# Turning the first mixer's tiles by DMA instead of on TensorE

## What is computed

```python
proj = h @ w_in                      # stick-breaking q,k,v; conv input (2 x 512); gla q,k,v,r; gates
w   = exp(log_sigmoid(z) + reverse_cumsum(log_keep) - log_keep)   # z = q k^T * 64**-0.5, 8 heads
sb  = w @ v                                                       # stick-breaking attention
u   = a * sigmoid(g);  y = depthwise_conv(u, conv_w)              # 31 taps over time, 512 channels
conv = silu(layer_norm(y))
S   = chunk_decay * S + k_dec^T v;  o = (q * 64**-0.5) @ S        # gated linear attention, 4 heads
gla = rms_norm(o) * silu(r)
m   = sum(sigmoid(gate_i) * (branch_i @ w_branch_i)) @ w_out
```

## Time and profile before

| | |
|---|---|
| median of 3 runs (lowest, highest) | 2055.99 us (2055.59, 2056.20) |
| the profiled execution, its own time | 2055.71 us |
| its span in the trace | 2053.9 us |
| busy: TensorE, VectorE, ScalarE | 2036.4, 1385.7, 1120.8 us |
| granted TensorE clock, mean | 0.999 |

### The profile page before, as it was taken

The page is one execution under the profiler, slowest core; times in us unless marked ns, Lnnn a source line. Parts: engine busy times, 40 slices in busy tenths (PEclk is TensorE's granted clock), DMA queues, the critical chain, the costliest instruction groups (busy, mean ns, idle before and its releaser), DMA issues.

```text
span 2053.9 us, 24653 instructions
## 1 busy us (share of the span) xinstructions
PE 2036.4 (99%) x9886; PEld 1683.2 (82%) x9886; DVE 1385.7 (67%) x1801; ACT 1120.8 (55%) x1386; POOL 0.2 (0%) x4
## 2 busy tenths in 40 slices
PE   8999999999999999999999999999999999999998
PEld 6888887888888888887888888898888888988887
DVE  6666798766657666798776656866665668566564
ACT  6445657664446445666564446646644466565443
POOL 0000000000000000000000000000000000000000
PEclk9999999999999999999999999999999999999999
DMA  8765654456766675554567655443576554445763
GB/s 273 210 205 170 208 177 145 167 193 203 217 200 205 208 212 169 196 171 144 180 212 211 212 175 200 164 145 135 179 219 206 181 197 156 149 143 186 204 217 113
DMA packets 302193, 382.69 MB, mean 186 GB/s; under 512 B 74672, under 2 KB 210176, under 8 KB 302080
## 3 DMA queue, kind: packets, MB, share of 16 engines
q1 hardware_dynamic: 298112, 369.88, 56.8%
q10 hardware_dynamic: 3968, 11.24, 1.6%
HBM read 365.86 MB, written 1.05 MB: 179 GB/s over the span
## 4 chain that ended last, share of the span: by engine, by line
PE 97%; DMA 1%; ACT 1%; DVE 1%; issue 0%; SPq 0%; DVEq 0%; ACTq 0%
PE ps L541 86%; PE ps L1072 2%; PE ps L609 1%; PE ps L632 1%; PE ps L1175 1%; PE ps L1156 1%; DMA raw<-in_ffn_w_up 1%; DVE x L1846 1%; PE ps L805 1%; DMA raw<-in_w_in 0%; PE ps L690 0%; PE ps L1020 0%; ACT w_hi L1234 0%; PE ps L986 0%; PE ps L650 0%
## 5 line engine op out<-in xcount | busy, mean ns | idle before, releaser
L1805 DVE TENSOR_TENSOR w_lo<-raw,w_hi 128x2048 fp32r<-128x2048 f32 x342 | 773.4, 2266 | 308.9 <-ACT w_hi L1234 307.7
L1234 ACT ACTIVATE w_hi<-raw 128x2048 fp32r<-128x2048 f32 x342 | 648.0, 1897 | 448.1 <-PE ps L541 327.2
L541 PE MATMUL ps<-w_hi,hT_hi 128*128 128x512 f32 x2000 | 788.9, 394 | 1.8 <-DVE w_lo L1805 1.8
L541 PE MATMUL ps<-w_lo,hT_hi 128*128 128x512 f32 x2000 | 779.7, 390 | 0.0
L541 PE MATMUL ps<-w_hi,hT_lo 128*128 128x512 f32 x2000 | 757.7, 391 | 0.0
L541 PEld LDWEIGHTS ps<-w_hi,hT_hi 128*128 128x128 f32 x2000 | 375.9, 188 | 83.9 <-issue 6.6
L541 PEld LDWEIGHTS ps<-w_hi,hT_lo 128*128 128x128 f32 x2000 | 375.2, 188 | 78.8
L541 PEld LDWEIGHTS ps<-w_lo,hT_hi 128*128 128x128 f32 x2000 | 376.1, 188 | 74.6
L541 PE MATMUL ps<-w_hi,bT_hi 128*128 128x512 f32 x640 | 250.9, 392 | 0.0
L541 PE MATMUL ps<-w_hi,bT_lo 128*128 128x512 f32 x640 | 249.3, 389 | 0.0
L541 PE MATMUL ps<-w_lo,bT_hi 128*128 128x512 f32 x640 | 249.2, 389 | 0.0
(11 more groups left out here) (298 smaller groups left out, 1312.6 us busy)
## 6 DMA issues: line engine op xcount, KB each, us to landing
raw<-in_w_in SPq DMA_DIRECT2D x160, 512.0 KB, 4.5
raw<-in_ffn_w_gate SPq DMA_DIRECT2D x88, 512.0 KB, 3.7
raw<-in_ffn_w_up SPq DMA_DIRECT2D x88, 512.0 KB, 4.7
raw<-in_ffn_w_down SPq DMA_DIRECT2D x88, 512.0 KB, 4.3
raw<-in_w_gate SPq DMA_DIRECT2D x44, 512.0 KB, 3.7
raw<-in_w_up SPq DMA_DIRECT2D x44, 512.0 KB, 4.7
raw<-in_w_down SPq DMA_DIRECT2D x44, 512.0 KB, 4.2
raw<-in_w_out SPq DMA_DIRECT2D x32, 512.0 KB, 4.4
```

The costliest lines, as they stand in the source:

```text
L541: mm = nc.tensor.matmul(bank(t, half), act[:, tiles[i], t * P:(t + 1) * P], w, start=start and (i, n) == steps[0], stop=stop and (i, n) == ...
L1234: nc.scalar.activation(w_hi[:, u % HIGH_RING, cols], raw[:, slot, cols], ACT.Copy).then_inc(high_ready, 1)
L1805: V.tensor_tensor(w_lo[:, slot, cols], raw[:, slot, cols], flat(w_hi[:, u % HIGH_RING, cols]), ALU.subtract).then_inc(low_ready, 1)
```

## The change

Three sets of tiles no longer pass through TensorE: the convolution's input, the linear attention's queries, and the stick-breaking queries and keys. VectorE parts each into 16-bit planes (`part_planes`), SP turns the planes with two DMA transposes (`turn_planes`, one for each `t`), and VectorE joins them (`join_planes`). Two transposes of 512 columns of 16 bits serve the linear attention's queries, as in the feed-forward blocks; the other three take two of 1024 columns. SP issues them in its load queue, after a wait for VectorE's planes. The scales that went with the copies out of PSUM (0.5 and 1/8) go into the evictions, by `rstd_half` and a new column `rstd_eighth`. The squares of the linear attention's output move from VectorE to ScalarE: eight Square activations of 128 columns with an accumulator, ahead of the root. Some taps change places on VectorE; their number is the same.

```diff
 SyncE, in the mixer's load loops (k is the unit after the one just issued)
+                    if k == U_FFN + 10:
+                        sp.wait_ge(*after("conv_glu", "planes", l))
+                        turn_planes(conv_planes_T, conv_planes, conv_turned)
+                    if k == U_FFN + 13:
+                        sp.wait_ge(*after("gla_decay", "planes", l))
+                        turn_planes(gq_planes_T, gq_planes, gla_q_turned)
...
+                        if k == U_FFN + 18:
+                            sp.wait_ge(*after("sb_planes", "q", l))
+                            turn_planes(sb_planes_T, sb_planes, sb_turned)
+                        if k == U_FFN + 20:
+                            sp.wait_ge(*after("sb_planes", "k", l))
+                            turn_planes(sb_planes_T, sb_planes, sb_turned)
 TensorE
-            steps = {("conv_g", 1): [gla_alpha], ("gla_qk", 0): [conv_turn], ("gla_v", 0): [gla_decays],
-                     ("gla_r", 0): [gla_updates], ("sb_q", 0): [gla_reads],
-                     ("sb_k", 0): [sb_turn_q], ("sb_k", 1): [gla_turn], ("sb_v", 0): [sb_turn_k]}
+            steps = {("conv_g", 1): [gla_alpha], ("gla_v", 0): [gla_decays], ("gla_r", 0): [gla_updates],
+                     ("sb_q", 0): [gla_reads], ("sb_k", 1): [gla_turn]}
 ScalarE
         def gla_std(l):
-            act.wait_ge(*after("gla_out", "sums", l))
+            act.wait_ge(*after("gla_out", "rows", l))
+            for h in range(8):
+                cols = slice(h * P, (h + 1) * P)
+                nc.scalar.activation(gsq_f[:, cols], go_f[:, cols], ACT.Square,
+                                     accum_out=ssg[:, h:h + 1]).then_inc(*done("gla_std", f"sum{h}"))
+            act.wait_ge(*after("gla_std", "sum7", l))
             nc.scalar.activation(stdg, ssg, ACT.Sqrt, bias=EPS, scale=1.0 / P).then_inc(*done("gla_std", "std"))
...
                 if name == "sb_k":
                     gla_std(l)
-                    act.wait_ge(*after("sb_turned", "q", l))
-                    copy(sbqT, two(4), "sb_in", "qT", 64 ** -0.5)
                 if name == "sb_v":
                     gla_out(l)
-                    act.wait_ge(*after("sb_turned", "k", l))
-                    copy(sbkT, two(4), "sb_in", "kT")
 VectorE
+        def part_planes(dst, src):
+
+            return V.tensor_copy(dst, src.bitcast(U16).rearrange("p t (n b) -> p t b n", b=2))
+
+        def join_planes(dst, src):
+
+
+            for t in range(TT):
+                joint = V.tensor_copy(dst.bitcast(U16).rearrange("p c (n b) -> p b c n", b=2)[:, :, :, t * P:(t + 1) * P],
+                                      src[:, t, :, :].rearrange("p (b c) n -> p b c n", b=2))
+            return joint
...
+        def sb_join(l, which):
+            dve.wait_ge(sb_turned, l * 64 + (32 if which == "q" else 64))
+            join_planes(sbqT if which == "q" else sbkT, sb_planes_T).then_inc(*done("sb_planes", which + "T"))
...
-            V.tensor_tensor(gsq_f, go_f, go_f, ALU.mult).then_inc(*done("gla_out", "squares"))
-            dve.wait_ge(*after("gla_out", "squares", l))
-            V.tensor_reduce(ssg, gsq_f.rearrange("p (h v) -> p h v", h=8), AX.X, ALU.add).then_inc(*done("gla_out", "sums"))
...
             weight_low(L, k + 9)
             conv_in(l)
-            taps(1)
+            taps(2)
             weight_low(L, k + 10)
+            gla_q_planes(l)
             taps(2)
...
             weight_low(L, k + 15)
             gla_rows(l)
+            sb_part(l, "q")
             weight_low(L, k + 16)
             gla_gated(l)
-            taps(2)
+            taps(1)
+            sb_join(l, "q")
             weight_low(L, k + 17)
+            sb_part(l, "k")
             taps(2)
             weight_low(L, k + 18)
-            taps(2)
+            sb_join(l, "k")
+            taps(1)
             weight_low(L, k + 19)
             gla_low(l)
-            taps(1)
+            taps(2)
```

More of the change, by code:

```diff
@@ L247, in _program @@
     joined = joined_f.rearrange("p (i t) -> p i t", i=2)
+    planes = lambda w: w.bitcast(U16).rearrange("p (t b n) -> p t b n", t=TT, b=2)
+    planes_T = lambda w: w.bitcast(U16).rearrange("p (t m n) -> p t m n", t=TT, n=P)
+    conv_planes, conv_planes_T = planes(merged_f[:, 0:1024]), planes_T(merged_f[:, 1024:2048])
+    sg_tail = sg[:, 1, :, :].rearrange("p t n -> p (t n)")
+    gq_planes, gq_planes_T = planes(sg_tail[:, 0:512]), planes_T(sg_tail[:, 512:1024])
+    sb_planes, sb_planes_T = planes(sg_tail), planes_T(pairbuf)
     gstate = sg[:, 0, :, :].rearrange("p t n -> p (t n)").rearrange("p (c n v) -> p c n v", c=2, n=4)
@@ L254, in _program @@
     conv_n = pairbuf.rearrange("p (t n) -> p t n", t=TT)
-    rstd_half = column(TT)
+    rstd_half, rstd_eighth = column(TT), column(TT)
     ssg, stdg, rstdg = column(8), column(8), column(8)
@@ L325, in _program @@
     halves_ready, halves_turned, hid_joined = sem("halves_ready"), sem("halves_turned"), sem("hid_joined")
+    conv_turned, gla_q_turned, sb_turned = sem("conv_u_turned"), sem("gla_q_turned"), sem("sb_qk_turned")
     gT_hi_ready, gT_ready = sem("gT_hi_ready"), sem("gT_ready")
@@ L455, in ffn, with turn_planes @@
             turn_halves(L, n, NCHUNK - 2)
+        def turn_planes(out, src, turned):
+            for t in range(TT):
+                sp.dma_start_transpose(out[:, t, :, :], src[:, t, :, :].rearrange("p b n -> p (b n)")).then_inc(turned, 16)
         for l in range(DEPTH):
@@ L704, in gla_decays @@
         def gla_decays(l):
[L706 to L712, removed]
             pe.wait_ge(*after("gla_keep", "softplus", l))
@@ L754, in gla_reads @@
             mm.then_inc(*done("gla_reads", "reads"))
[L756 to L764, removed]
         def gla_turn(l):
             pe.wait_ge(*after("gla_out", "gated", l))
-            pe.wait_ge(*after("conv_glu", "u", l))
             turn(go_f.rearrange("p (t n) -> p t n", t=TT), 6).then_inc(*done("gla_out_turned", "turned"))
[L771 to L774, removed]
         def sb_logits(l, c):
-            pe.wait_ge(*after("sb_in", "kT", l))
+            pe.wait_ge(*after("sb_planes", "kT", l))
             if c:
                 pe.wait_ge(*after("sb_keep", f"copied{c - 1}", l))
+            else:
+                pe.wait_ge(*after("gla_out", "rows", l))
             heads = [(e, slice(64 * e, 64 * e + 64)) for e in range(2)]
@@ L1366, in rows @@
         def rows(dst, src, stage, step, func=ACT.Copy):
-            scale = rstd_half if func == ACT.Tanh else rstd_in
+            scale = rstd_half if func == ACT.Tanh or step == "a" else rstd_eighth if (stage, step) == ("sb_in", "q") else rstd_in
             for t in range(TT):
@@ L1466, in mixer_a @@
                     rms_ready(L, 1)
-                if name == "conv_g":
-                    act.wait_ge(*after("tanh_scale", "half", l))
+                if name == "conv_a":
+                    act.wait_ge(*after("tanh_scale", "eighth", l))
                 if name == "gla_qk":
@@ L1484, in mixer_a @@
                 if name == "sb_q":
-                    act.wait_ge(*after("conv_turned", "u", l))
+                    act.wait_ge(*after("conv_glu", "planes", l))
                 if name == "sb_v":
@@ L1965, in gla_keep, with gla_q_planes, sb_part @@
             V.tensor_tensor(nla, nla, gdec, ALU.add).then_inc(*done("gla_keep", "softplus"))
+        def part_planes(dst, src):
+            return V.tensor_copy(dst, src.bitcast(U16).rearrange("p t (n b) -> p t b n", b=2))
+        def join_planes(dst, src):
+            for t in range(TT):
+                joint = V.tensor_copy(dst.bitcast(U16).rearrange("p c (n b) -> p b c n", b=2)[:, :, :, t * P:(t + 1) * P],
+                                      src[:, t, :, :].rearrange("p (b c) n -> p b c n", b=2))
+            return joint
+        def gla_q_planes(l):
+            dve.wait_ge(*after("gla_in", "qk", l))
+            part_planes(gq_planes, gqk[:, :, 0:256]).then_inc(*done("gla_decay", "planes"))
+        def sb_part(l, which):
+            dve.wait_ge(*after("sb_in", which, l))
+            part_planes(sb_planes, sb_q if which == "q" else sb_k).then_inc(*done("sb_planes", which))
+        def sb_join(l, which):
+            dve.wait_ge(sb_turned, l * 64 + (32 if which == "q" else 64))
+            join_planes(sbqT if which == "q" else sbkT, sb_planes_T).then_inc(*done("sb_planes", which + "T"))
         def gla_keys(l):
-            dve.wait_ge(*after("gla_turned", "q", l))
-            V.tensor_copy(gqT, ps[:, 6, :].rearrange("p (c t) -> p c t", c=2)).then_inc(*done("gla_decay", "q"))
+            dve.wait_ge(gla_q_turned, l * 32 + 32)
+            join_planes(gqT, gq_planes_T).then_inc(*done("gla_decay", "q"))
             dve.wait_ge(*after("gla_exp", "to_end", l))
@@ L2021, in conv_glu @@
             V.scalar_tensor_tensor(conv_u, conv_s, 1.0, conv_u, ALU.add, ALU.mult).then_inc(*done("conv_glu", "glu"))
+            dve.wait_ge(*after("conv_glu", "glu", l))
```

(6 more changed lines are left out.)

## The result

The changed kernel takes 2063.78 us (median of 5, 2062.99 to 2064.74) against 2055.59 for the one before (5 runs, 2054.48 to 2056.20): ratio 1.0039, 95% interval 1.0028 to 1.0051. It is slower by 8 us, on the forecast side and inside the range; the forecast was 2066.4. The profiled execution has a span of 2062.0 us, 8.1 more than before.

A forecast was written before the change was run, and what follows sets the result against it. TensorE was taken to bound the kernel. A late first softplus delays it 3.55 us a layer and slow clock costs 1.67: (3.55 + 1.67) x 2 = 10.4 us slower, 2066.4 us, range 2058.5 to 2071.

The forecast's parts named there:

- What bounds the kernel: Whole kernel: TensorE sets the end; VectorE's first softplus is ready only 0.35 us before TensorE's first sums need it.
- The turns' price: Mixer, TensorE: transposes taken away free 0.87 us per set of eight, 3.05 us a layer, 6.1 in all.
- The squares: Linear attention's output, ScalarE: eight squares take 3.1 us, 0.39 each; root ends at 280.65, `gla_gated` ends 1.12 us later.
- VectorE's queue: VectorE from the end of `gla_gated` to the first softplus: one tap less, added parting and joinings, 30.2 us.
- The transposes of the keys: Stick-breaking keys, DMA on SP: 6.3 us until they land, so VectorE waits 0.9 us; bounds 0 and 2.2.
- The clock: TensorE behind each stall: one episode at half clock, 1.67 us lost; bounds none and two episodes.
- The sum: Both layers: 3.55 us later sums plus 1.67 of slow clock, times 2, 10.4 us slower, median 2066.4.
- Stall without loss of clock: First sums: TensorE stalls but keeps its clock; 2063.1 us, or 2061.3 without a wait for the transposes; chance 0.24.
- the sign: TensorE ahead of the first sums in each layer: a gap of 5 to 8 us, released by VectorE's softplus.
- The heavier case: Longer stall or slow clock, from slower transposes, a Square table load or two slow stretches; 2069 to 2072.5; chance 0.14.
- the even one: VectorE's copies much cheaper, at half price, without clock loss, so the change is nearly even: 2057.7 us; chance 0.11.
- the faster one: VectorE's first softplus comes in time, by 308.65, so 6.1 us are gained: 2049.9 us; chance 0.06.

The follow-up runs named there:

- the run with the filler: Changed kernel plus seven extra float32 matmuls of 384 columns on constants, ahead of TensorE's wait for the first softplus; 2059.28 us, ratio 1.0019.
- the two early tiles: Kernel before with only the convolution's input and the linear attention's queries turned by DMA; 2053.82 us, ratio 0.9991.

## Why the prediction was right

**What bounds the kernel.** Right. TensorE sets the end, and what counts was the margin of 0.35 us at the first sums; the only new wait of TensorE of any size is there, in both layers. With the taps out of the way the loss is gone, with TensorE kept busy the slow clock is gone, and each run took away the part that it was meant to.

**The turns' price.** 3.05 us a layer were predicted and 3.14 measured. The version with the taps moved shows them as a gain, 84.95 us from the mark to the sums for 88.09.

**The squares.** The mechanism held, the size was too large: one Square with its accumulator takes 0.29 us from start to start, not the 0.39 of the Exp that served as the nearest row. That Exp also reads a bias from `stat`, which the Square does not; whether the 0.1 us is that operand or the function, no run separates. The root ended at 280.06 for 280.65, or 0.8 earlier if the mark's 0.23 is taken off. No table load came for Square. It was also right that the squares' leaving would only become idle time on VectorE, and the run with the squares alone shows that this part of the change costs time.

**VectorE's queue.** 30.2 us were predicted from the end of `gla_gated` to the end of the softplus, and 312.67 - 282.57 = 30.1 measured. Parting was 1.14 us from start to start for 1.1, a joining 1.26 to 1.28 for 1.28.

**The transposes of the keys.** This is the term that was wrong in kind: a wait was put in where there is none. I took SP's issue as proportional to columns, 5.0 us for the pair; it is 2.62 us (288.87), as for half the columns. VectorE did not wait for the keys: the 0.9 us fall away. The rule of the Trainium skill (Advanced Engine Details and Errata, X-Bar Transpose), by which there would be no wait, gave the better answer: 1.8 us less over both layers. By it alone the sum would have been 2064.6. The trace agrees in so far as the pair, issued at 288.87, was there when VectorE asked at 294.13, and the mixer's transposes landed 3.4 us after their issue in the median, for 4.6 of a 512 KB load.

**The clock.** 1.67 us an episode were taken from the start of the kernel; 2.26 and 1.71 were measured, and the run with the filler, 4.5 us faster by the medians, bears it out. The stall of 4.94 us is shorter than the 6.6 forecast, and one episode came with each. The Trainium skill (TensorE: Matmul & The Clock Gate, Part 1) has the same cause: the clock goes by how busy TensorE has been of late. The trace agrees: the clock is at one half from within the first layer's stall, and full again after work has been going on.

**The sum.** Predicted 3.55 + 1.67 = 5.22 us a layer, measured 1.80 + 2.0 = 3.8 in the mean of both. The sums were forecast 1.75 us too late in each layer: 0.8 for the squares, 0.9 for the wait that did not come and 0.1 for VectorE's queue. The turns gave 0.1 more than forecast; that makes the stall longer and leaves the sums where they are. The clock was taken 0.3 too cheap. Over both layers the sums were 3.5 us too late in the forecast. The clock, forecast too cheap, and the start of the kernel made up for 0.8 of that, and that part of the closeness is luck.

**The rivals.** Stall without loss of clock (2061.3 to 2063.1) came nearer in time than the forecast: 2063.78 is 0.7 from its upper end, 2.6 from 2066.4, and 0.2 below the range of its own (2064 to 2069) that the forecast was given. The time alone would speak for this rival; it is the stretches and the filler that refute it, since the slow clock is there and costs 3.7 to 4.0 us. The stall, 4.8 us in the list, is also a little under the "5 to 8" named as the sign, and well over the 3 us that would have refuted the forecast. The heavier case, the even one and the faster one did not occur. As for the faster one, the point from which it would decide was right; what it took was not cheaper copies but other work out of the way, which the change did not do.

What stays open: why the start of the kernel varies by 1.7 us from one profiled execution to another. It limits what a median can tell: the two early tiles gain 1.6 us in the median where the two mixers of their trace gain 2.7, which is inside the interval. Why a stall of 3.1 us cost the clock and one of 3.3 us did not is open too.

## What to carry to other kernels

Work that is taken off the engine that sets the end is gained only if the engine that takes it over does not become late with what it delivers next. The two early tiles, which VectorE handles where it has idle time, gave their 1.35 us a layer; the turns of queries and keys lie in the stretch where VectorE is full, and together with the later root of ScalarE they made the stall. So look for the row pair with the smallest margin between "ready" and "asked for", and reckon both sides of it with the change. Ask of each side whether it moves along when the first engine gets earlier: ScalarE's chain here did, VectorE's queue did not. A filler that nobody waits for yet (here the taps) belongs behind such a point, not ahead of it: with four taps a layer moved, the same change went from 8 us slower to 5 us faster. A stall of several microseconds of TensorE costs more than its length where the engine comes back at half clock.

## What the runs showed of the hardware

- A DMA transpose of a 128 x 1024 tile of 16 bits keeps SP as long as one of 128 x 512: 2.62 us for two against 2.50.
- A Square of 128 x 128 with accumulator takes 0.29 us on ScalarE from start to start, where an Exp of the same shape that also reads a bias from `stat` takes 0.39.
- Behind stalls of 4.9 us TensorE's granted clock was 0.50, and it came back after some 3.3 and 4.5 us of new work, at a loss of 1.7 and 2.3 us. Of two stalls of 3.1 and 3.3 us, the first cost 3.07 us more, with the clock back after about 6 us, and the other 0.1; those of 0.9 us left the clock at 1.00 and cost 0.1 more.
- Parting 128 x 1024 float32 into 16-bit planes and joining them again cost VectorE 1.14 and 1.26 to 1.28 us, while TensorE turned the same tile in 0.87 us.
